# DeltaNet units: another order on VectorE, and the odd unit's third low weight part moved to VectorE

## What is computed

```python
qkv = jax.nn.silu(causal_conv(jnp.concatenate([dq, dk, dv], axis=-1), conv_w))   # 4 taps
dq = l2norm(dq) * (DN_DK ** -0.5); dk = l2norm(dk)
L = jnp.where(strict, einsum('bhncd,bhnjd->bhncj', k_beta, k) * decay, 0.0)
sol = lax.linalg.triangular_solve(L + eye, rhs, left_side=True, lower=True)
v_new = u_n - einsum('bhcd,bhde->bhce', w_n, state)
o = einsum('bhcd,bhde->bhce', q_n, state) + einsum('bhcj,bhje->bhce', attn_n, v_new)
state = state * exp(gl) + einsum('bhcd,bhce->bhde', k_n, v_new)
```

## Time and profile before

| | us |
|---|---|
| median of 3 runs | 2652.01 (2651.72 to 2652.16) |
| profiled execution, whole | 2653.16 |
| its span | 2651.3 |
| TensorE busy | 2631.7 (99%) |
| VectorE busy | 1730.4 (65%) |
| GpSimd busy | 819.1 (31%) |
| ScalarE busy | 699.6 (26%) |

### The profile page before, as it was taken

How to read it: one execution, slowest core, us unless ns; L and a number is a source line. 1 busy time by engine, 2 the same in 40 slices (tenths; PEclk the granted TensorE clock), 3 DMA queues, 4 the chain that set the end, 5 groups by cost and what they waited for, 6 DMA issues and landing times.

```text
span 2651.3 us, 40106 instructions
## 1 busy us (share of the span) xinstructions
PE 2631.7 (99%) x14874; PEld 2248.4 (85%) x14874; DVE 1730.4 (65%) x3868; ACT 699.6 (26%) x1408; POOL 819.1 (31%) x451
## 2 busy tenths in 40 slices
PE   8999999999999999999999999999999999999998
PEld 6888888888898899888878888888888998898887
DVE  7878777877755655434578778777877555553333
ACT  5333333333312222200143333333232211231001
POOL 3223333333312212434512333333323122132453
PEclk9999999999999999999999999999999999999999
DMA  5321323122211112433533222222222111133344
GB/s 174 98 85 53 85 65 89 53 85 65 85 42 51 34 41 73 129 95 117 164 91 97 67 78 64 73 77 70 68 73 77 43 50 42 41 106 100 99 136 151
DMA packets 293413, 217.77 MB, mean 82 GB/s; under 512 B 31746, under 2 KB 246100, under 8 KB 292964
## 3 DMA queue, kind: packets, MB, share of 16 engines
q1 hardware_dynamic: 259620, 159.07, 20.8%
q10 hardware_dynamic: 33600, 56.15, 6.3%
HBM read 176.30 MB, written 38.86 MB: 81 GB/s over the span
## 4 chain that ended last, share of the span: by engine, by line
PE 91%; DVE 4%; DMA 2%; issue 1%; ACT 1%; SPq 1%; POOL 0%; DVEq 0%; ACTq 0%
PE dense_ps L852 22%; PE dense_ps L856 22%; PE dense_ps L854 22%; PE work L835 3%; PE dense_ps L876 2%; PE dense_ps L877 2%; PE dense_ps L878 2%; PE work L1133 1%; DMA arena<-l_scratch 1%; PE work L1170 1%; PE work L1107 1%; PE work L1190 1%; PE work L1090 1%; PE work L1159 1%; PE work L1183 1%
## 5 line engine op out<-in xcount | busy, mean ns | idle before, releaser
L852 PE MATMUL dense_ps<-act_hi,w_hi 128*128 128x512 f32 x2552 | 1048.2, 411 | 0.8 <-POOL act_lo L2580 0.7
L856 PE MATMUL dense_ps<-act_hi,w_lo 128*128 128x512 f32 x2552 | 999.0, 391 | 0.0
L854 PE MATMUL dense_ps<-act_lo,w_hi 128*128 128x512 f32 x2552 | 997.1, 391 | 0.0
L2559 POOL TENSOR_TENSOR w_lo<-w_raw,w_hi 128x1024 fp32r<-128x1024 f32 x162 | 399.9, 2469 | 1005.2 <-ACT w_hi L1417 563.4
L856 PEld LDWEIGHTS dense_ps<-act_hi,w_lo 128*128 128x128 f32 x2552 | 479.0, 188 | 106.1
L852 PEld LDWEIGHTS dense_ps<-act_hi,w_hi 128*128 128x128 f32 x2552 | 481.0, 188 | 84.9 <-POOL act_lo L2580 2.3
L854 PEld LDWEIGHTS dense_ps<-act_lo,w_hi 128*128 128x128 f32 x2552 | 481.4, 189 | 79.1 <-issue 0.5
L1959 DVE SCALAR_TENSOR_TENSOR arena<-arena,cols 128x512 f32<-128x512 f32 x288 | 241.0, 837 | 5.2
L1417 ACT ACTIVATE w_hi<-w_raw 128x1024 fp32r<-128x1024 f32 x94 | 99.1, 1055 | 329.8 <-PE dense_ps L856 310.5
L1407 ACT ACTIVATE arena<-dense_ps 128x512 f32<-128x512 f32 x96 | 57.3, 597 | 267.0 <-PE dense_ps L856 267.0
L1973 DVE SCALAR_TENSOR_TENSOR arena<-arena 128x512 f32<-128x512 f32 x96 | 112.5, 1172 | 11.9 <-ACT arena L1423 11.4
(11 more groups left out here) (259 smaller groups left out, 4016.5 us busy)
## 6 DMA issues: line engine op xcount, KB each, us to landing
w_raw<-in_w_in SPq DMA_DIRECT2D x138, 512.0 KB, 3.8
arena<-l_scratch SPq DMA_DIRECT2D x64, 256.0 KB
arena<-gate_scratch ACTq DMA_DIRECT2D x64, 256.0 KB, 2.9
gate_scratch<-arena ACTq DMA_DIRECT2D x36, 256.0 KB, 2.0
w_raw<-in_w_out SPq DMA_DIRECT2D x18, 512.0 KB, 3.9
o_scratch<-arena ACTq DMA_DIRECT2D x32, 256.0 KB, 2.0
w_raw<-in_w_up_dn SPq DMA_DIRECT2D x16, 512.0 KB, 3.9
arena<-o_scratch ACTq DMA_DIRECT2D x32, 256.0 KB, 3.6
```

Source lines behind the costliest of these rows:

```text
L852: eng.matmul(dense_ps[:, to, :], w_hi[:, slot, k, :], hi[:, k, seg], start=(k == 0), stop=False)
L854: eng.matmul(dense_ps[:, to, :], w_hi[:, slot, k, :], lo[:, k, seg], start=False, stop=False)
L856: mm = eng.matmul(dense_ps[:, to, :], w_lo[:, slot, k, :], hi[:, k, seg], start=False, stop=(k == KT - 1))
L2559: eng.tensor_tensor(w_lo[:, slot, :, :], w_from[second][:, :, :], w_hi[:, slot, :, :].bitcast(F32), ALU.subtract)\
```

## The change

Three things are changed in the list of steps, and one in GpSimd's program. `qe` goes from slot 5 to slot 10 (behind `xu` 3) in all units but "first" and "odd_last". In "even" and "odd" units `spread` gives no taps to the slots 12 or 13 to 16 and more to the last ones; `tanh` and `silu` of part 0 (even) and part 4 (odd) get places of their own. In "odd" units `low 2` is added at slot 19, and GpSimd leaves this low part out.

```diff
@@ unit_schedule
-        at(5, "qe")
+        at(10, "qe")
@@
+    if kind == "even":
+        at(13, "tanh", 0)
+        at(14, "silu", 0)
+    if kind == "odd":
+        at(19, "low", 2)
+        at(14, "tanh", 4)
+        at(16, "silu", 4)
@@
     def taps(i):
-        return [("conv", i, k) for k in range(TAPS)] + [("tanh", i)]
+        placed = kind == "even" and i == 0 or kind == "odd" and i == 4
+        return [("conv", i, k) for k in range(TAPS)] + ([] if placed else [("tanh", i)])
@@
+        elif kind in ("even", "odd"):
+            spread(0 if 3 <= n < 8 or (12 if kind == "even" else 13) <= n < 17 else 2 if n in (12, 17) or n > 17 else 1)
         else:
             spread(0 if 3 <= n < 8 else 1 if n < 18 and n not in (12, 16) else 2)
@@ gpsimd, delta_unit
-                            elif kind != "first" and not is_v(idx):
+                            elif kind != "first" and not is_v(idx) and not (kind == "odd" and step[1] == 2):
                                 split_w(g + idx, idx % 2)
```

## The result

The changed kernel took 2672.2 us (median of 4 runs, 2668.48 to 2673.25) against 2652.09 (4 runs, 2651.72 to 2652.67): ratio 1.007, 95% interval 1.0058 to 1.0081. It is 20.1 us slower; 8.3 had been forecast. The profiled execution took 2673.25 us around its span of 2671.4, at a granted clock of 0.998 (0.999 before).

A forecast was written before the change was run, and what follows sets the result against it. TensorE, busy 2631.7 of 2651.3 us, was taken as the bound. Losses of 9 x 0.46 + 5.1 + 3.6 = 12.8 us less wins of 2.3 and 2.2 made +8.3 on 2652.0: 2660.3 us, range 2652 to 2669.

The forecast's parts named there:

- Even unit's middle, 2.3 us won: Even unit: `level_x` 1 ends some 0.7 us sooner, so TensorE's weight loads stop waiting for it; 2.3 us won.
- `qe`, 2.2 us won: `qe`, 0.79 us, leaves VectorE's stretch between `so` 1 and `ks` 2, ending today's late `xu`; some 2.2 us won.
- The low part 2.05 us later: Odd unit: VectorE's low part ends at 449.85, 2.05 us after GpSimd's, moving SyncE's stores and block loads as much.
- Issue to solving 6.3 us: Time from block loads' issue to the first solving step, taken as 6.3 us in ordinary units; the step trusted least.
- the bound of 6.58: Upper bound, 6.58 us, on issue to first solving step, from units that do not wait; gives 0.74 us late.
- The three late units 5.1: Three of 12 even units whose block load is late already: stalls of 1.9, 1.9 and about 1.3, 5.1 us lost.
- the last even ones 3.6: Each layer's last even unit, with `z_silu` 0 between solving and `so` 1: 2.1 and 1.5, 3.6 us lost.
- The read-back did not keep its room: Rival, chance 0.14: block loads still land in time, ordinary stalls vanish; if all vanish, 4.5 us won, 2647.5.
- the net stay small: Rival, chance 0.18: loads land at 5.9 us and only the late units stall; +4.2 us, 2656.
- the threshold of 1.3: Delay of the low part, about 1.3 us, at which it is decided whether the read-back keeps its room.
- VectorE's backlog: Rival, chance 0.12: taps at the even unit's end make `xu` 0 of 12 odd units wait 0.5 us; 2666.
- The lock-out: Rival: `silu` 5, freed from GpSimd's lock, gets 1.04 us back per odd unit, TensorE nothing; 2647.5 at best, no own chance.

The follow-up runs named there:

- e8: Kernel before with VectorE's new order alone, the low part staying on GpSimd and `qe` at slot 5: 2648.76 us.
- e1: Changed kernel with the odd unit's third low part given back to GpSimd, new order and `qe` at slot 10 kept: 2649.2 us.
- e10: Changed kernel with SyncE waiting until the block loads have landed, ahead of the gates' stores, in 12 of 14 pairs: 2656.42 us.
- e13: Changed kernel with SyncE waiting until the block loads have landed, but behind the gates' two stores, in 12 of 14 pairs: 2663.33 us.
- e2: Kernel before with the low part alone moved to VectorE at slot 19, order and `qe` as before: 2673.99 us.
- e5: Changed kernel with VectorE's low part placed ahead of `vt`, still behind the four taps: 2661.22 us.
- e6: Changed kernel with VectorE's low part placed behind `silu` 5, at slot 21: 2704.26 us.

## Why the prediction was wrong in size

The direction, the place and the chain were right; the time (20.1 us lost for 8.3) lay above the range. Step by step:

*Even unit's middle, 2.3 us won:* right. The excess over 0.23 us in the distance of matmul starts at this place, summed over all units, fell from 3.1 to 0.6 us, 2.5 won.

*`qe`, 2.2 us won:* wrong step. The new order with `qe` left at slot 5 (e8) is as fast as with it at 10 (e1): 2648.8 and 2649.2, on two chips. The stalls, 1.8 us before, are 1.5 in e8's trace and 0.4 in e1's, one execution each, so that at most 1 us of the 2.2 is `qe`'s. That the sum of the wins came out is partly luck. All wins together were put at 4.5; e1 shows 4.4 against the kernel before on its chip (2653.6).

*The low part 2.05 us later:* measured 1.97, from -12.75 to -10.78. Right. Not seen was that the new order would have given GpSimd's another 0.5 us, so that against e1 it is 2.5 late.

*Issue to solving 6.3 us:* this term failed, and it is the largest part of the miss. It was right for the kernel from which it was taken: by the completion records (5.62 us from the second issue in the nine ordinary units, 0.64 between the issues, 0.09 from landing to solving) it was 6.35 there, well under the bound of 6.58. The failed step is that it was carried over as a constant. In the changed kernel the same nine units took 6.9 (mean), and over all twelve the landing went from 5.85 to 6.28; it was 5.8 in the e10 unit shown and 7.2 in that of the changed kernel. It depends on what is issued behind the loads; what lengthened it from before to changed is open (e13). With the issue 0.1 later than forecast, and `ks` 2 0.14 behind `so` 1 for 0.06, it makes 1.17 us a unit for 0.46: 10.5 us for 4.1.

*The three late units 5.1, the last even ones 3.6:* measured 7.4 and 6.1. The shape was right; the latest unit lost 4.2 for 1.9, as its second load was issued 7.6 us after the low part, where 6.0 is usual, and landed in 7.1, and 0.6 are the clock. In the second layer's last even unit (3.95 for 2.1) the second load was issued 7.1 us after the low part, for 6.0 in that unit before, and 0.7 are the clock. That the clock could fall behind a long wait was in no term.
Sum: 24.0 for 12.8, less the 4 won.

*Rivals.* The read-back did not keep its room, nor did the net stay small: the ordinary units alone stall 10.5 us. By the records of the kernel before, its nine ordinary units would have borne 1.2 to 1.9 us of delay (1.6 on average) with an unchanged flight, so the threshold of 1.3 was near; but with the landing at 6.04 `ks` 2 waits seven times in e2 at a delay of 1.22, and e5, 1.38 us later than before (-11.37), stalls 11 us. VectorE's backlog at the even unit's end cost nothing that shows: no `xu` 0 or `so` 0 of an odd unit waits for it. The lock-out was as told: `silu` 5 now takes 0.69 us (the row at 451.18) for 1.72 in the earlier trace rows, and TensorE gets nothing for it. At the even unit's end the first tap was held, as forecast, though it has one tensor input only, until 0.28 us after GpSimd's low part (492.30 to 494.70):

```profile
493.36 1.62 DVE L1966 TENSOR_SCALAR arena<-arena,cols 128x512 f32<-128x512 f32 x1
```

*Range.* Its 1.24 us a unit should have been 1.14 (0.74 and the 0.4), which lowers the end of 2669 by less than 1. The upper end took the flight at 6.58, a bound from units at rest, as the worst case. A wait put on every unit should have been priced with the flight of the late units too, 7.8 by the earlier trace rows.

## What to carry over

When work that releases a queue is moved, price the queue behind it, and multiply: here 2 us of lateness of one instruction became 23, because nine of the 14 units had about 1.6 us of room and the others 0.7 or less, and because the flight time is no constant. Order a queue by who needs it first; a store that is ready should not stand behind a load that waits, and a load that is waited for should not be followed at once by transfers that nobody is waiting for. An engine with 35% idle time takes work for free only at a place where nobody is waiting yet when it ends: the same instruction 3.4 us earlier cost nothing.

## What was not expected of the hardware

- Two 256 KB stores issued 0.6 us behind two 256 KB loads, on the same queue, lengthened their landing from 5.05 to 5.89 us (e10, e13; twelve units each).
- TensorE's granted clock was 0.5 in stretches behind some of its waits of 1.9 to 3.9 us (two in the changed kernel, eight in e6), so that a wait cost up to 1.45 us more than its length. The page's mean over the span, 0.998, hides this.
- In eight of the fifteen profiled executions the issue of one to three block stores took 1.2 to 1.7 us for the usual 0.43 (in the SyncE rows of the changed kernel, eight stores in 4.60 us, for 3.81 in that unit before). It is part of why two units took 6.9 and 7.6 us from the low part to the second load, where 6.0 is usual; in others, as the last even unit of the second layer (7.1), the stores were issued on time and landed late. What causes either was not tried.
- A GpSimd instruction on 128 x 4 elements took 1.45 or 1.01 us in the same place of the odd unit, before and after VectorE's order changed (13 and 14 of 14 units). Before, two of VectorE's taps ran beside it (443.81 to 445.34); what stretches it was not tried.
